# First stage of a hybrid decoder layer: two more buffers for raw weights, another order of the low parts, and products of ones on TensorE

## The reference

```python
h = rmsnorm(x, norm1_g)
z = h @ w_in            # c_q | c_kv | k_rope | gMLP u (512) | gMLP v (512)
zg = gelu(z[..., OFF_G:])
u = zg[..., :GMLP_WIDTH]
v = layernorm(zg[..., GMLP_WIDTH:], v_norm_g, v_norm_b)
...
g = spatial_gate(u, v, w_spatial, b_spatial)
o = attend(...)         # latent attention, prompt and paged cache
x = x + concat([rmsnorm(a), rmsnorm(g)]) @ w_out
x = x + (silu(h2 @ w_gate) * (h2 @ w_up)) @ w_down
y = rmsnorm(x, final_norm_g)
```

## Time and profile before

| | |
|---|---|
| three executions | 1358.76, 1359.56, 1365.93 us (median 1359.56) |
| the profiled execution | 1362.44 us, of which the span in the profile is 1360.7 us |
| TensorE busy | 1308.5 us, 96% of the span |
| VectorE, ScalarE, GpSimd busy | 60%, 38%, 32% |
| mean granted TensorE clock | 0.986 |

### The profile page before, as it was taken

How to read it: one execution, slowest core, us unless ns; L and a number is a source line. 1 busy time by engine, 2 the same in 40 slices (tenths; PEclk the granted TensorE clock), 3 DMA queues, 4 the chain that set the end, 5 groups by cost and what they waited for, 6 DMA issues and landing times.

```text
span 1360.7 us, 23850 instructions
## 1 busy us (share of the span) xinstructions
PE 1308.5 (96%) x9362; PEld 1226.2 (90%) x9362; DVE 821.2 (60%) x1241; ACT 513.0 (38%) x902; POOL 429.2 (32%) x279
## 2 busy tenths in 40 slices
PE   6999999999999998999999999999999999999997
PEld 4788988888888558999899999999999999999987
DVE  4874056666666338167944553445535468899976
ACT  5423224566566414113422222222222234444451
POOL 2633335442433115652044444444443400000000
PEclk9999999999999899899999999999999999999998
DMA  8421101000015444641212222122222189757503
GB/s 286 160 60 31 36 17 58 20 17 5 16 66 191 155 163 155 222 133 49 67 69 80 79 74 83 63 79 79 86 73 74 68 304 339 259 189 246 173 1 131
DMA packets 70345, 151.58 MB, mean 111 GB/s; under 512 B 9106, under 2 KB 16658, under 8 KB 69810
## 3 DMA queue, kind: packets, MB, share of 16 engines
q1 hardware_dynamic: 70258, 150.39, 32.4%
HBM read 127.80 MB, written 22.56 MB: 111 GB/s over the span
## 4 chain that ended last, share of the span: by engine, by line
PE 80%; DVE 8%; issue 5%; DMA 3%; ACT 2%; POOL 2%; SPq 0%; POOLq 0%; DVEq 0%; ACTq 0%
PE ps L983 24%; PE ps L984 24%; PE ps L985 24%; PE ps L1199 2%; DMA araw<-in_w_dn 2%; PE ps L1265 1%; DVE x L2082 1%; PE ps L991 1%; DMA ab<-acts 1%; PE ps L1310 1%; POOL rt L782 1%; DVE mL L2446 1%; DVE hL L2136 1%; PE ps L1275 1%; DVE aHL L2757 0%
## 5 line engine op out<-in xcount | busy, mean ns | idle before, releaser
L952 POOL TENSOR_TENSOR ws<-wraw,ws 128x1024 fp32r<-128x1024 f32 x50 | 125.2, 2504 | 215.8 <-ACT ws L1568 215.8
L983 PE MATMUL ps<-bHL,aHL 128*128 128x272 f32 x616 | 178.7, 290 | 6.3 <-DVE bHL L2760 6.1
L985 PE MATMUL ps<-bHL,aHL 128*128 128x272 f32 x616 | 177.3, 288 | 0.0
L984 PE MATMUL ps<-bHL,aHL 128*128 128x272 f32 x616 | 177.2, 288 | 0.0
L2603 DVE TENSOR_TENSOR bufP<-bufP,ps 128x544 f32<-128x544 f32 x66 | 47.4, 721 | 133.7 <-PE ps L985 131.4
L1568 ACT ACTIVATE ws<-wraw 128x1024 fp32r<-128x1024 f32 x55 | 58.4, 1061 | 174.2 <-PE ps L985 168.9
L983 PEld LDWEIGHTS ps<-bHL,aHL 128*128 128x128 f32 x616 | 116.0, 188 | 8.1 <-DVE bHL L2760 8.0
L984 PEld LDWEIGHTS ps<-bHL,aHL 128*128 128x128 f32 x616 | 116.0, 188 | 0.0
L985 PEld LDWEIGHTS ps<-bHL,aHL 128*128 128x128 f32 x616 | 116.0, 188 | 0.0
L975 POOL TENSOR_TENSOR rt<-ms,mhalf 128x3 f32<-128x3 f32 (+1 forms) x3 | 3.0, 998 | 255.1 <-DVE ms L2790 255.1
L2336 DVE TENSOR_TENSOR pTL<-ps,pTH 128x512 fp32r<-128x512 f32 (+1 forms) x96 | 53.2, 555 | 44.3 <-ACT pTH L1568 43.4
(11 more groups left out here) (371 smaller groups left out, 4521.3 us busy)
## 6 DMA issues: line engine op xcount, KB each, us to landing
araw<-in_w_dn SPq DMA_DIRECT2D x121, 256.0 KB, 3.6
wraw<-in_w_gu SPq DMA_DIRECT2D x44, 512.0 KB, 3.5
cp<-in_cache SPq DMA_DIRECT2D x64, 272.0 KB, 4.5
ab<-acts SPq DMA_DIRECT2D x34, 272.0 KB, 4.5
raw<-in_w_out SPq DMA_DIRECT2D x16, 512.0 KB, 4.1
acts<-bufC SPq DMA_DIRECT2D x22, 272.0 KB, 2.1
xt<-in_x_tok SPq DMA_DIRECT2D x9, 512.0 KB, 6.7
x<-x2s SPq DMA_DIRECT2D x8, 544.0 KB, 6.1
```

The lines of the kernel that those rows point to most:

```text
L952: pool.tensor_tensor(w[:, 1, :], w_source(j), w[:, 0, :], ALU.subtract).then_inc(cw_lo, 1)
L983: nc.tensor.matmul(out, wh, xh, start=start, stop=False)
L984: nc.tensor.matmul(out, wh, xl, start=False, stop=False)
L985: return nc.tensor.matmul(out, wl, xh, start=False, stop=stop)
```

## The change

- Weight pieces 2 and 3 go into a buffer of their own, `raw_more`, which lies on the memory of `xt` 0 and 1. SyncE issues them without a wait, directly behind pieces 0 and 1 and ahead of x piece 1. They count on the semaphores of `xt` 0 and 1.
- `xt` 2 is loaded ahead of `xt` 0 and 1; these two now wait for the low part of piece 2, and of piece 3 (`split_lo`).
- VectorE makes the low parts in the order in which tile 0 uses them: for each j, `hL` of the first column piece for k = 2j and 2j + 1, then `vwL` j. The whole second column piece follows, then the third.
- TensorE gets products of ones with ones, 128 x 128 in plain float32, into a bank of PSUM that nothing reads: 14 when `ones` is made, 6 after x piece 0 has landed, 3 after the first `vwH`.

```diff
@@ -220,6 +225,7 @@
         raw = Region(R0).put("raw", [P, 2, 1024])
         xt = Region(X0, nc.sbuf_usable_end).put("xt", [P, 3, D])
+        raw_more = Region(X0).put("raw_more", [P, 2, 1024])
@@ -505,6 +511,10 @@
+        def raw_of(n):
+
+            return raw_more[:, n % 2, :] if N_V + 2 <= n < N_SP else raw[:, n % 2, :]
@@ -527,6 +537,8 @@
                 if b >= 3:
                     sp_.wait_ge(n1_sq, b - 2)
+                elif b < 2:
+                    sp_.wait_ge(split_lo, N_V + 3 + b)
@@ -534,12 +546,13 @@
             piece(N_V, d["w_v"][0])
             piece(N_V + 1, d["w_v"][1])
+            for j in (2, 3):
+                sp_.dma_start(raw_of(N_V + j), d["w_v"][j]).then_inc(ld_xt[j % 2], 16)
             load_x(1)
-            piece(N_V + 2, d["w_v"][2])
-            piece(N_V + 3, d["w_v"][3])
             load_x(2)
-            for b in range(3):
-                load_xt(b)
+            load_xt(2)
+            load_xt(0)
+            load_xt(1)
             load_x(3)
@@ -755,8 +768,11 @@
-                r = raw[:, n % 2, 0:width]
-                pool.wait_ge(raw_full[n % 2], 16 * (n // 2 + 1))
+                r = raw_of(n)[:, 0:width]
+                if N_V + 2 <= n < N_SP:
+                    pool.wait_ge(ld_xt[n % 2], 16)
+                else:
+                    pool.wait_ge(raw_full[n % 2], raw_count(n))
@@ -1001,7 +1017,17 @@
+            def keep_busy(bank, times):
+
+                for _ in range(times):
+                    nc.tensor.matmul(ps[:, bank, 0:P], ones[:, :], ones[:, :], start=True, stop=True)
+
             pe.wait_ge(made, 1)
+            keep_busy(7, 14)
+            pe.wait_ge(ld_x[0], 16)
+            keep_busy(7, 6)
+            pe.wait_ge(split_hi, 1)
+            keep_busy(7, 3)
@@ -2142,15 +2168,10 @@
-            low1(0, range(2))
-            weights_lo(N_V, gw(vwL, 0), gw(vwH, 0))
-            low1(0, range(2, KD))
-            for j in range(1, 4):
+            for j in range(4):
+                low1(0, range(2 * j, 2 * j + 2))
                 weights_lo(N_V + j, gw(vwL, j), gw(vwH, j))
-                if j == 1:
-                    low1(1, range(4))
-                elif j == 2:
-                    low1(1, range(4, KD))
+            low1(1)
             low1(2)
```

More of the change, by code:

```diff
@@ L120, in xt_of, with raw_count @@
     return t if t < NT - 1 else XT - 1
+def raw_count(n):
+    return 16 * (n // 2 + (n < 2))
 def offsets(n):
@@ L803, in spatial_weights @@
             def spatial_weights():
-                pool.wait_ge(raw_full[N_SP % 2], 16 * (N_SP // 2 + 1))
+                pool.wait_ge(raw_full[N_SP % 2], raw_count(N_SP))
                 rsp = raw[:, N_SP % 2, :].rearrange("p (g i) -> p g i", g=G)
@@ L1582, in square_rows @@
                 m = xt_rows(b)
-                act.wait_ge(ld_xt[b % 3], 16 * (b // 3 + 1))
+                act.wait_ge(ld_xt[b % 3], 16 * (b // 3 + 1 + (b % 3 < 2)))
                 nc.scalar.activation(xt[0:m, b % 3, :], xt[0:m, b % 3, :], ACT.Square,
@@ L2129, in weights_lo @@
                 dve.wait_ge(split_hi, n + 1)
-                nc.vector.tensor_tensor(lo, raw[:, n % 2, :], hi, ALU.subtract).then_inc(split_lo, 1)
+                nc.vector.tensor_tensor(lo, raw_of(n), hi, ALU.subtract).then_inc(split_lo, 1)
             def low1(c, ks=range(KD)):
```

## The result

The changed kernel takes 1352.75 us (median of 7 executions, 1348.95 to 1355.60), the kernel before 1359.56 (7 executions, 1357.44 to 1365.93). That is 6.8 us or 0.5% less by the medians. The ratio of all executions is 0.9941, 0.6% less, with a 95% interval from 0.9918 to 0.9963. The forecast was 1354.3, range 1349.5 to 1359.8. The profiled execution took 1350.68 us, its span is 1348.8. In one execution of a kernel further on, of 1820.9 us, the core was in a slower state (granted clock 0.653), and it stays out of that kernel's times and ratio.

A forecast was written before the change was run, and what follows sets the result against it. VectorE, never pausing from 9.12 us and blocking with GpSimd, was taken to bound tile 0; 2.6 us from the chain, 2.4 from the clock and 0.3 from the hand-over make 5.3: 1359.56 - 5.3 = 1354.3 us, range 1349.5 to 1359.8.

The forecast's parts named there:

- What bounded the first stage: Tile 0: VectorE, without pause from 9.12 us, sets TensorE's groups; only six of its 14 low parts of x belong there.
- The two engines block each other: Start of the kernel: VectorE and GpSimd do not work at the same time; last low part at 18.2 us, without blocking 15.3.
- The sum of 9.2 us: VectorE and GpSimd from 9.12 us: low parts of weights 4.6, three copies 3.0, six low parts of x 1.6 us.
- The second x piece and the `xt` loads cost nothing: Transfers: x piece moves from 12.07 to about 14.6 us, not wanted before about 18; the queue does not run dry.
- The products of ones do not delay the operands, and bring the clock up: TensorE before tile 0: clock up at about 6.3 us, products end at about 9.9, before the operands at 10.35.
- Rival B: Tile 0: the clock does not stay up; groups take 2.56 us, gain 3.3 us, 1356.3 us; chance 0.18.
- the sum's 2.4 us for the last 12 products: TensorE, first 30 products: the last 12 at the low clock each gain 0.2 us by running at 0.23 us.
- The sum of 5.3 us: TensorE's 30th product done at 21.0 instead of 26.3 us: 2.6 from the chain, 2.4 from the clock, 0.3 from the hand-over.
- Everything behind moves up 5.3 us on TensorE: After tile 0: the whole gain carries on; first u product at 63.2 us instead of 68.50, without a wait.
- rival D: Middle of the kernel: the shift changes stretches at the low clock; two more make it slower, +4.9 us, 1364.5; chance 0.08.

The follow-up runs named there:

- a kernel further on: The changed kernel with 92 waiting instructions in place of the products of ones; ratio to the kernel before 0.9937 (0.9913 to 0.9961), other nine executions 1348.3 to 1356.0 us.

## Why the prediction was right, point by point

- **What bounded the first stage.** Right: VectorE, with low parts that tile 0 does not need yet. Order alone moved the last low part by 1.6 us, and the buffers alone by nothing.
- **The two engines block each other.** Right in kind, shown by taking it away. The sum of 9.2 us was off little: from the first copy, the last low part was to end after 10.1 us (18.2 less 8.04) and ended after 9.8 (17.37 less 7.53). The other 0.5 us of the difference between 18.2 and 17.4 is that the first copy came sooner in that profile. The blocking cost VectorE 2.5 us, where the sum has 3.0 for the three copies.
- **The second x piece and the `xt` loads cost nothing.** Right: 14.26 against 14.6, no wait for the third x piece or for `xt`.
- **The products of ones do not delay the operands, and bring the clock up.** They did not delay the operands: the first product came 0.4 us late through the copy of piece 1. The clock rose at 4.2 us, before the 6.3 forecast. I held that it would stay up through tile 0; it did not in either profile of the changed kernel. Rival B was right about that and wrong about its price. In the first profile the low clock fell on group 1, which had 3.2 us until VectorE's next low part; the sum's 2.4 us for the last 12 products came in nearly in full.
- **The sum of 5.3 us.** In the first stage 5.4 us (60.5 to 55.0) in one profile and 4.5 in the other. It is made differently than I had it: without the products of ones 4.0 us of it remain, since with the waits between the groups short or gone (1.11 us ahead of group 2, none behind it) the clock comes up by itself at 19.1. The sum's 2.4 us for the clock were thus mostly not the work of the products of ones: leaving these out cost the first stage 1.5 us against one profile and 0.5 against the other.
- **The step that failed** is the one from the first stage to the whole: "Everything behind moves up 5.3 us on TensorE", with the later clock (rival D) as the only thing that could change it. Measured were 6.8 us by the medians and 8 to 9 by the ratios, against 4.5 to 5.4 in the first stage. What the runs showed in its place is the fetching of code: in the profiles of kernels with 92 more instructions 1.1 to 2.2 us at 680, and likely the like later. That the whole still fell into the range, and near the forecast, is in part luck: the gain from the code, 3 us or more by the ratios, has nothing to do with the sum.

Near 1100 us the same switch shows. Between VectorE's 887th and 912th instruction (1090.7 and 1114.3 us before) all kernels with 92 to 121 added instructions took 21.3 to 22.2 us, and all others, that with 256 among them, 23.4 to 24.4. One transfer there is the 2720 KB of `ab<-acts`, for which ScalarE waits, in the kernel before (issued at 1087.49) and in that with 92 waiting instructions (issued at 1080.22):

```profile
1098.64 0.66 ACT L1568 ACTIVATE bHL<-ab 128x544 fp32r<-128x544 f32 x1 [2.81 <-DMA ab<-acts]
1090.68 0.66 ACT L1570 ACTIVATE bHL<-ab 128x544 fp32r<-128x544 f32 x1 [2.14 <-DMA ab<-acts]
```

In the five kernels with none or 256 more instructions a code transfer starts 4.8 to 5.2 us behind its issue, and ScalarE starts 11.1 to 11.3 us behind it; in the other seven and the changed kernel's first profile no code transfer starts within 12 us behind it, and ScalarE starts after 9.7 to 10.7. That is about 1 us.

Open: the rest of the step of 3.0 us near 1100. And whether products of ones are worth anything to the whole cannot be told from these runs: by the first stage 0.5 to 1.5 us, by the ratio against idle instructions 0.0 +- 0.3% (4 us).

## What to carry to other kernels

Put the operands in the order in which the engine that bounds the kernel takes them, and read the list of who blocks whom before buying buffers: here the order alone took 4.1 us off the first stage, the buffers on top of it at most 1, and giving an idle third engine the copies brought the last low part another 2.5 us forward. When an edit adds or removes instructions on an engine with long straight code, measure it against a kernel with as many idle instructions: some 90 of them, doing nothing, changed this one by 0.4%. And where the gain that the profile shows at the place of the edit (0.5 us with the products of ones alone) is far from the gain on the whole, that is a reason to compare the traces at the same instruction all the way down.

## What the hardware showed that I had not expected

- TensorE's code comes in transfers of 16 KB, one for 256 instructions (92 more moved them by 5.3 to 5.9 of some 16.2 us, 256 brought them back), and they disturb those of the data. The one near 680 us took 0.94 to 1.74 us, and a 512 KB transfer that met it ended 4.7 to 5.6 us behind its issue instead of 3.1 to 3.4.
- An instruction of TensorE that only waits for a semaphore already reached costs about 0.11 us (256 of them: from 1 to 28.95 us).
- The same kernel got the high clock at other places of its first stage in two profiles: from 4.2 us with a fall from 11.0 to 14.5, and from 5.9 us with a fall from 16.1 to 19.5. That alone made 1.0 us of its first stage.
